# Next-stage weight loads issued before the last result rows, at two mixture-of-experts exits

## What is computed

```
def _hier_moe(t, wr_g, br_g, wr_e, br_e, w_gate, w_up, w_down):
    ...
    def expert_block(args):
        x_blk, e = args
        hidden = jax.nn.silu(x_blk @ w_gate[e]) * (x_blk @ w_up[e])
        return hidden @ w_down[e]
```

## Time and profile before

| | us |
|---|---|
| three runs | 2678.81, 2679.42, 2680.64 |
| median | 2679.42 |
| the profiled execution, its own time | 2681.68 |
| its span, first to last instruction | 2679.7 |
| mean granted TensorE clock | 0.974 of full speed |

### The profile page before, as it was taken

The page is one execution under the profiler, slowest core; times in us unless marked ns, Lnnn a source line. Parts: engine busy times, 40 slices in busy tenths (PEclk is TensorE's granted clock), DMA queues, the critical chain, the costliest instruction groups (busy, mean ns, idle before and its releaser), DMA issues. The chain is left out here.

```text
span 2679.7 us, 32556 instructions
## 1 busy us (share of the span) xinstructions
PE 2369.0 (88%) x12819; PEld 1396.0 (52%) x12819; DVE 1233.1 (46%) x2419; ACT 569.2 (21%) x1327; POOL 169.7 (6%) x272
## 2 busy tenths in 40 slices
PE   7999898988987778798998997778789899999999
PEld 4456566455553334345656553334344675888444
DVE  3367776754222222466554332222335653545565
ACT  3000477210100000115541100000122562111000
POOL 0000000001111111000001211111000000000000
PEclk9999999998999999999997999999999999999999
DMA  8773400629999999713028999999820112222643
GB/s 298 273 275 128 173 1 2 230 96 410 424 425 425 425 425 425 289 67 113 1 90 357 424 424 426 425 424 425 322 103 0 52 65 78 63 92 66 219 157 125
DMA packets 133236, 619.39 MB, mean 231 GB/s; under 512 B 21232, under 2 KB 48152, under 8 KB 103384
## 3 DMA queue, kind: packets, MB, share of 16 engines
q1 hardware_dynamic: 122520, 596.24, 55.9%
q0 software_dynamic: 10560, 21.01, 2.0%
HBM read 600.34 MB, written 30.47 MB: 235 GB/s over the span
## 5 line engine op out<-in xcount | busy, mean ns | idle before, releaser
L2282 PE MATMUL moe_gate<-moe_wg,moe_xg_t 128*64 128x256 f32 x1984 | 243.3, 396 | 50.7 <-DMA moe_wg<-in_moe_w_gate 49.2
L2328 PE MATMUL moe_down<-moe_wd,moe_hid_t 128*64 128x512 f32 x1024 | 235.5, 601 | 43.9 <-DMA moe_wd<-in_moe_w_down 31.4
L2282 PE MATMUL moe_up<-moe_wu,moe_xg_t 128*64 128x256 f32 x1984 | 237.7, 390 | 41.3 <-DMA moe_wu<-in_moe_w_up 41.2
L2282 PEld LDWEIGHTS moe_gate<-moe_wg,moe_xg_t 128*64 128x64 f32 x1984 | 148.5, 137 | 163.0 <-DMA moe_wg<-in_moe_w_gate 82.7
L2282 PEld LDWEIGHTS moe_up<-moe_wu,moe_xg_t 128*64 128x64 f32 x1984 | 145.2, 134 | 129.4 <-DMA moe_wu<-in_moe_w_up 59.9
L3656 PE MATMUL mlp_acc<-m_h,mlp_w 128*128 128x256 f32 x896 | 196.3, 382 | 5.3 <-DVE c_buffer L3833 2.5
L3656 PEld LDWEIGHTS mlp_acc<-m_h,mlp_w 128*128 128x128 f32 x896 | 171.0, 191 | 30.4 <-issue 4.1
L2513 DVE COPY moe_y<-moe_down 128x512 f32<-128x512 f32 x62 | 42.9, 691 | 308.2 <-PE moe_down L2328 308.2
L2328 PEld LDWEIGHTS moe_down<-moe_wd,moe_hid_t 128*64 128x64 f32 x1024 | 73.8, 137 | 161.5 <-issue 123.4
L1791 PE MATMUL out_acc<-out_w,out_o_t 128*128 128x512 f32 x320 | 144.5, 608 | 4.1 <-ACT out_o_t L1636 4.1
L2500 DVE TENSOR_SCALAR moe_sig<-moe_sig 128x256 f32<-128x256 f32 x62 | 18.2, 294 | 271.4 <-ACT moe_sig L2376 271.4
(11 more groups left out here) (557 smaller groups left out, 3581.0 us busy)
## 6 DMA issues: line engine op xcount, KB each, us to landing
moe_wg<-in_moe_w_gate SPq DMA_DIRECT2D x64, 2048.0 KB, 42.2
moe_wu<-in_moe_w_up SPq DMA_DIRECT2D x64, 2048.0 KB, 42.2
moe_wd<-in_moe_w_down SPq DMA_DIRECT2D x64, 2048.0 KB, 42.3
qkv_mod_w<-in_mod_w SPq DMA_DIRECT2D x42, 1024.0 KB, 6.3
mlp_w<-in_w_down SPq DMA_DIRECT2D x44, 512.0 KB, 5.6
mlp_w<-in_w_up SPq DMA_DIRECT2D x16, 1024.0 KB, 8.0
qkv_w<-in_a_w_qkv SPq DMA_DIRECT2D x12, 1024.0 KB, 10.6
m_h<-in_w_down SPq DMA_DIRECT2D x20, 512.0 KB, 6.1
```

Of the source, the lines that this page charges most:

```text
L2282: mm = nc.tensor.matmul(acc[b][halves[f], 0:HF], x_t[:, k, c, :], w[:, c, k, :].rearrange("p (q f j) -> p f q j", f=2, j=2)[:, f], start=( ...
L2328: mm = nc.tensor.matmul(down[b][halves[c], :], hid_t[:, k, h, :], wd[z][:, 2 * h + k, c * NCHUNK:(c + 1) * NCHUNK], start=(k, h) == (0, 0) ...
```

## The change

Chunk 0 of the next projection is issued between the last expert's weights and the gates and rows of the expert phase, after a wait for the gate matmuls of expert 30 (the last reader of gate slot 0). In layer 0 it leaves its place among the norm vectors. In layer 1 the chunks 1 to 4 go from the next phase to the place right behind the result rows.

```
@@ enter_1_loads / enter_2_loads
         sp.dma_start(add[:, x, :], bcast_rows(shift)).then_inc(ring["vec_in"][x], 16)
-        if x == 0:
-            load_chunk(sp, ring, e["b_w_qkv"][0], [NCHUNK] * 3, 0)
+
+def first_load_1(e, ring, sp):
+    load_chunk(sp, ring, e["b_w_qkv"][0], [NCHUNK] * 3, 0)
+
+def first_load_2(e, ring, sp):
+    load_chunk(sp, ring, e["w_in_2"][0], IN2_WIDTHS, 0)

 def enter_2_loads(e, ring, sp):
-    load_chunk(sp, ring, e["w_in_2"][0], IN2_WIDTHS, 0)
+    for c in range(1, len(IN2_WIDTHS)):
+        load_chunk(sp, ring, e["w_in_2"][0], IN2_WIDTHS, c)
@@ experts(..., early_loads, next_loads), SP
             while_left(sp, nx, n, two_extra)
+            sp.wait_ge(s["gated"], last + (n + 1) // 2 * 2)
+            early_loads(e, ring, sp)
             sp.wait_ge(s["downed"], last + (n + 1) // 2 * 2)
             sp.dma_start(gates, bcast_rows(mod_part(e, layer, 5)(0))).then_inc(s["gates_in"], 16)
@@ enter_block_2, SP
-            load_chunk(sp, ring, e["w_in_2"][0], IN2_WIDTHS, 1)
             sp.wait_ge(ring["last_out"], 16)
             sp.dma_start(ys, src[TC + 1]).then_inc(s["y_in"], 16)
             sp.dma_start(gates, bcast_rows(mod_part(e, 1, 5)(0))).then_inc(s["gates_in"], 16)
-            load_chunk(sp, ring, e["w_in_2"][0], IN2_WIDTHS, 2)
...
-            for c in range(3, n_chunks):
-                load_chunk(sp, ring, e["w_in_2"][0], IN2_WIDTHS, c)
             for i in range(2, TX):
```

More of the change, by code:

```diff
@@ L2076, in while_left, with experts @@
                 one(i2)
-def experts(nc, e, layer, tiles, r, ring, head, next_loads):
+def experts(nc, e, layer, tiles, r, ring, head, early_loads, next_loads):
     nt = len(tiles)
@@ L2615, in layer_0 @@
         route(nc, e, 0, tiles, logits, r, ring)
-        experts(nc, e, 0, tiles, r, ring, TC, enter_1_loads)
+        experts(nc, e, 0, tiles, r, ring, TC, first_load_1, enter_1_loads)
     logits_scope.close()
@@ L2868, in layer_1 @@
         route(nc, e, 1, stream, logits, r, ring)
-        experts(nc, e, 1, stream, r, ring, TC, enter_2_loads)
+        experts(nc, e, 1, stream, r, ring, TC, first_load_2, enter_2_loads)
     logits_scope.close()
```

## The result

| | before | changed |
|---|---|---|
| median, us | 2680.22 | 2685.73 |
| executions | 12 (2678.06 to 2687.11) | 12 (2681.25 to 2701.59) |
| ratio to before | | 1.0032 [1.0017, 1.0046] |

The changed kernel measured 0.3% slower, where no change was forecast. The ratio is not that of the two medians, which is 1.0021; it weighs all executions, and here it is that of their means (2689.43 and 2680.78 us). The executions of the changed kernel fall in two groups: seven from 2681.25 to 2686.87 us, and five from 2694.14 to 2701.59 us, whose mean granted clock is 0.967 or less (0.970 to 0.974 in the seven). The profiled execution is one of the five: 2694.14 us of its own, span 2692.2 us.

The account below looks back on a forecast made before the run. TensorE was busy 88% of the span; late result rows bounded the handovers. Terms 8.9 - 2.4 - 8.6 + 1.4 = -0.7 us, applied to the 2679.42 us median, gave 2678.7 us, range 2672.5 to 2686.0.

Parts of the forecast that it names:

- Chunk 0 ahead of the rows: Both handovers: result rows land 4.4 and 4.5 us later behind chunk 0 and the gates, costing 8.9 us.
- The rival in which the rows lose half: Both handovers: idle engines carry most of chunk 0, rows late by 2.2 us each, 2674.2 us; chance 0.20 for half or less.
- The added wait on SP: Expert phases: SP waits for expert 30's gate matmuls where it waited idle anyhow; cost 0 (0 to 0.5 us).
- First handover, what comes back: Projection 1: gates land 1.6 us sooner and a slow chunk half recovers, 0.8; gain 2.4 us (0 to 3.6).
- Second handover, the stall: Projection 2: TensorE's stall on chunk 3 goes, gain 8.6 us; second tile's gates one or two us late without cost.
- SP's four issues: Second handover: SP, freed at 1925.8, holds the phase's end past DVE's last operation; cost 1.4 us (0 to 7.9).
- No change forecast: Whole kernel: sum of -0.7 us, 2678.7 us, counted as no change; chance 0.71 of landing within 0.2%.
- the bound of 0.2%: Whole kernel: about 0.2% (5.4 us) is what a measurement can tell from no change.
- the rivals: Handovers: rows lose half or less (0.20), SP holds the second phase's end (0.15), stall returns in projection 2 (0.07).
- neither sign that was to make the prediction wrong: Handovers: rows landing within 2 us of where they were, or the second projection phase starting after 1930.

Follow-up runs that it names:

- the kernel before a third time: The kernel before, nothing edited, run once more as a kernel of its own: 2681.53 us, ratio 0.9997.
- experiment 3: Against the kernel before, only chunk 0 ahead of the rows in both handovers, block 2's chunks 1 to 4 left in the next phase: 2691.28 us, ratio 1.0038.
- experiment 4: Against the kernel before, no early chunk, block 2's chunks 0 to 4 all issued behind the rows: 2679.23 us, ratio 1.0007.
- experiment 5: Against the changed kernel, chunk 1 also put ahead of the rows in the second handover: 2687.07 us in one execution.
- experiment 8: Against the kernel before, block 2's chunks 0 to 2 behind the rows, chunks 3 and 4 in the next phase: 2675.54 us, ratio 0.9977.
- experiment 10: Against the kernel before, block 2's chunks 0 to 2 behind the rows, plus 24 useless transposes in block 2's attention openings: 2671.05 us, ratio 0.9956.
- the two repeats: The changed kernel measured twice more, nothing edited, against the kernel before: 2682.02 us, ratio 1.0015, and 2683.19 us, ratio 1.0006.
- experiment 2: The kernel before, nothing edited, run as a kernel of its own against itself: 2682.38 us, ratio 1.0020.

## Why the prediction was wrong

The handovers add up close to what was forecast. Means over the four profiles with the change and the four of the kernel before (table above; the transposes lie behind these stages):

| step | forecast | measured |
|---|---|---|
| first expert phase (rows late) | +4.4 | 499.54 - 495.46 = +4.1 |
| projection 1 (what comes back) | -2.4 | 124.67 - 124.25 = +0.4 |
| second expert phase (rows late, SP) | +4.5 + 1.4 | 496.33 - 491.42 = +4.9 |
| projection 2 (stall gone) | -8.6 | 168.35 - 176.71 = -8.4 |

With -0.5 us in the unchanged stages between, it is +0.5 us where -0.7 was forecast.

- **Chunk 0 ahead of the rows**: right, 4.3 and 4.6 us against 4.4 and 4.5 in the profiled execution, and 4.2 and 4.9 between the means of four profiles each. As in the sum, that is less than the 5.4 us of a whole chunk: in the kernel before the engines were no longer full when the rows were issued (share 0.50). One chunk more costs 4.9 to 5.5 us. By the 358 GB/s of the Trainium skill ("DMA: Bandwidth & Descriptors", "Where 436 GB/s comes from") 2 MB would have taken 5.9 us; the runs lie below that. The rival in which the rows lose half is refuted.
- **The added wait on SP**: right, nobody waited for it. It did put the gates' issue behind chunk 0, which had not landed, and that issue held SP for 8.44 us; without harm, since the scatters landed later.
- **First handover, what comes back**: this step failed; over four profiles each its term is +0.4 us instead of -2.4, and over all thirteen profiles projection 1 takes 124.4 us with chunk 0 ahead of the rows and without. The wait did shrink in the profiled execution, from 1.98 to 0.20 us, and projection 1 took 2.1 us less, as if the step were right. But before's profiled execution was one of two kinds that the same code shows. Its gates come after 11.03 us of DVE's idle time and TensorE waits 1.98 us; in the kernel before a third time it is 9.50 and 0.45:

```profile
1120.42 0.75 DVE L2726 TENSOR_SCALAR qkv_ys<-qkv_ys,r_weight 128x1024 f32<-128x1024 f32 x1 [9.50 <-DMA moe_wu<-mod_scratch]
...
1127.31 0.66 PE L2808 MATMUL qkv_tp<-ident_sb,qkv_stage 128*128 128x128 f32 x4 [0.45 <-DVE qkv_stage L203]
```

The change has both kinds too (projection 1 of 123.9 and of 126.9 us). One row of one execution was taken for an effect of the queue. And the changed kernel lost about 1.2 us again near the end of projection 1: behind an idle time of 3.17 us TensorE ran at 1.2 GHz (granted 0.50 from 1219 to 1221). All four profiles with the change show this, of the kernel before one of four; but with the first handovers of experiments 3, 4, 5, 8 and 10 it is 5 of 6 against 3 of 7, too few to tie it to the change. The changed kernel's row, and the same one of the kernel before a third time:

```profile
1217.84 1.60 PE L2808 MATMUL qkv_n_tp<-ident_sb,qkv_h 128*128 128x128 f32 x8 [3.17 <-DVE qkv_h L2754]
```

```profile
1216.78 1.09 PE L2799 MATMUL qkv_n_tp<-ident_sb,qkv_h 128*128 128x128 f32 x8 [3.17 <-DVE qkv_h L2745]
```

- **Second handover, the stall**: right, 8.4 us. The second tile's gates arrive at 1944.34, 16.6 us after the end of the expert phase's last operation, where before took 14.9; that is the 1.7 us late that the step allowed for, and TensorE didn't wait for them.
- **SP's four issues**: forecast 1.4 us, measured 0; the term was mis-sized. DMA issues of the changed kernel, of the first three loads behind the rows (size, us to landing):

```profile
moe_wu<-in_w_in SPq DMA_DIRECT2D x1, 2048.0 KB, 14.4
moe_wd<-in_w_in SPq DMA_DIRECT2D x1, 2048.0 KB, 19.3
moe_wg<-in_w_in SPq DMA_DIRECT2D x1, 2048.0 KB, 20.4
```

Chunk 2 lands at 1910.85 + 19.3 = 1930.2, chunk 3 at 1915.54 + 20.4 = 1935.9. SP was free at 1926.7, 9.2 us before that, where the step had 6.5, and 1.0 us before DVE's last operation ended (1927.7). It is the fifth load behind rows that are on time that costs: 4.3 us in experiment 4.

- **No change forecast, 1.0032 measured**: the step that failed is the bound of 0.2% for what a measurement of this kernel can tell from no change. The prediction gives no working for it, and had three runs within 1.8 us. The kernel has a second group of executions, some 15 us longer, that the three runs and the profile of before did not show; with 12 executions their number moves the median and, still more, the ratio: identical code came out at 1.0020 [1.0002, 1.0038]. None of the rivals held this, because all were looked for in the stages that the change touches, and neither sign that was to make the prediction wrong came up (rows 4.3 and 4.6 us late; the second projection phase began at 1928.3). In the first measurement 5 of 12 were long, and of the 8.7 us between the means they make 6.0. The other seven have a mean 2.6 us above before (median 2682.7, 2.5 above); in the two repeats the executions that are not long have means 0.0 and 0.8 us above the compared ones. That some small part of the 2.6 us is the change's own isn't ruled out: its stages add up to +0.5.

## What to carry to other kernels

A load put ahead of one that the path waits for costs most or all of its transfer when the queues are full (4.2 to 5.5 us of 5.4 here); put behind it, it costs nothing until the issuing engine is held past the phase's end, so spread such loads over both sides of that meeting. Before a small difference is explained, the unchanged kernel must be measured in the changed one's place, and the executions looked at one by one: two groups of times with two mean clocks are no matter of the edit until it is shown. When stages are compared between two profiles, a difference of 1 to 3 us in one row needs a second profile of the same code.

## What the runs showed of the hardware

- In three of ten profiled executions without the added transposes TensorE fell to 1.2 GHz for 30.7 to 34.1 us in a row at the start of block 2's attention, although it was busy without a gap meanwhile, and then went back to 2.4 GHz for the rest of it. In a fourth (experiment 2) it fell there too, but for some us only (window 2118 to 2120 at 0.50, attention 83.7 us). Before the fall it had stood idle between its first score matmuls for moments of 0.73 us and the like; these are in executions that don't fall, too:

```profile
2113.92 1.13 PE L3435 MATMUL att_score<-c_k,c_q 64*128 64x256 f32 x8 [1.04 <-PEq L132]
2115.79 1.92 PE L3435 MATMUL att_score<-c_k,c_q 96*128 96x256 f32 x4 [0.73 <-DVE att_neg_top L3493]
```

```profile
2116.64 1.13 PE L3430 MATMUL att_score<-c_k,c_q 96*128 96x256 f32 x4 [0.73 <-DVE att_neg_top L3488]
```

The first fence is the changed kernel's timeline: the second group is already at half clock (1.92 us for four matmuls). The second is before's same group with the same idle time before it, at full clock (1.13 us).

- One DMA issue of 512 KB held SP for 8.44 us in the first handover and 5.58 us in the second, behind 2 MB loads that had not been worked off; with two chunks ahead, the issue of the second chunk held it for 10.62 us. Not every issue behind a load under way is held: that of the rows took 0.37 us in the first handover (1088.79), 5.5 us before chunk 0 had landed (1067.20 + 27.1 = 1094.3).
